# Two attentions: the split of one weight chunk moved behind the rotary embedding, and a value transposition moved ahead

## The chip, the cores and the metric

One Trainium2 chip, one NeuronCore of it. The metric is the device time of one execution in microseconds (us). The engines are named as in the profile: PE is TensorE's matmul, PEld its weight load, DVE is VectorE, ACT ScalarE, POOL GpSimd, and SP the engine that issues nearly all DMAs, one after the other. Each engine works through its own list of instructions in order and waits on semaphores where it needs another's result.

## What is computed

A decoder step of four layers for 256 prompt tokens and 64 sample tokens that share all weights (320 columns, 1024 features, float32). Each layer is a SwiGLU network, a token mixer, and another SwiGLU network, each behind an RMS norm. The mixers are a chunked gMLP, a sliding-window attention with sinks, a short convolution, and a sparse attention. The two attentions matter here:

```python
q = _rope(qkv[..., :qd]...)          # sliding-window attention: 16 heads, 2 key/value heads
k = _rope(qkv[..., qd:qd + kvd]...)
o, ... = _band_attn(q, k, v, window=128, sinks)
x = x + o @ w_o

proj = xn @ w_in                     # sparse attention
q, kv4, kvw, gates = ...             # kv4: k_cmp, v_cmp, k_sel, v_sel; kvw: k_win, v_win
q_rot = _rope(q); k_sel = _rope(k_sel); k_win = _rope(k_win)
o = gates0 * o_cmp(q) + gates1 * o_sel(q_rot) + gates2 * o_win(q_rot)
x = x + o @ w_o
```

For the samples, the sparse attention reads its past selected keys and values from a paged cache (8 pages for each of 8 sequences) and the last 128 window rows from another.

## The kernel before

All matrices of weights arrive as chunks of 1024 x 256 in one stream. SP loads chunk n into one of two slots of `w_raw` (L264), but only after the slot's former chunk, n - 2, has been split: `sp_chunk` waits on `lo_ready`. The split makes float32 out of two rounded parts: ACT copies a half chunk to `w_hi` (`act_split`, L290), DVE subtracts it from the raw values into `w_lo` (`dve_split`, L299, two instructions a chunk, one a half). PE then makes three products for each of eight row tiles of a half (`pe_half`, L317). ACT and DVE run two chunks ahead: while PE multiplies with chunk c of a stage, they split chunk c + 2. So in the last two chunks of an attention's input projection they split the first and the second chunk of the output projection (`mix_out`).

The projection of an attention (`pe_in_turning`, `dve_in_turning`) interleaves the rotary embedding with the chunks. DVE evacuates both halves of chunk c (`dve_take3`, L933), splits chunk c + 2, and then rotates the tiles of chunk c - 1 (`turned`). One rotation is: POOL multiplies by the cosine (L928), PE multiplies by a permutation into bank 5 or 6 (L884), DVE multiplies that by the sine (L907) and adds the cosine part (L910). After the last chunk two rotations of the chunk before it and two of its own are left.

After the projection come rounds: eight heads' pairs and eight sequences (`rounds`), in each of which three units u = 0, 1, 2 (two prompt tiles, one sequence) are scored, masked, exponentiated, turned and multiplied with values. POOL stages the queries (L1225 to L1239, L2025 to L2029) once the last rotation is through, PE makes the scores (L1066; L1687 to L1700), DVE masks them (from L1170; from L1899).

In the sparse attention PE, behind the last rotation, waits until DVE has read banks 5 and 6 (`rot_sin`), transposes the prompt's and the samples' new values of two branches into them (L1672, six transpositions), ACT copies them out (L1790, L1791), and PE waits for these copies (`nv_ready`) before its first scores. The gates and the compressed keys and values are laid out earlier with banks 7 and 4 (`lay`; DVE signals its end with five steps of `n_lay_step`).

SP's list around the sparse attention is: the eight chunks of `nsa_in`, the four chunks of `mix_out` (the fourth, chunk 3, waits for the split of the second, chunk 1), then `sp_nsa_store`: the window caches `n_wk` (L1601) and `n_wv` (L1602), then in a loop eight page numbers out of SBUF (L1607) and eight page loads into `n_sel` (L1611), for one sequence after the other. PE's unit u = 2 needs `n_wk` and `n_wv` from L1693 on and the pages from L1700 on. In the sliding-window attention the caches are loaded before the chunks of `mix_out`.

Of the kernel before, what the change touches and what calls it, by code (L numbers as in the profile page):

```python
# [10 lines left out]
ACT = mybir.ActivationFunctionType  # L11
# [3 lines left out]
P = 128  # L15
# [3 lines left out]
NS_TOK = 64  # L19
# [13 lines left out]
RAW = 2  # L33
# [73 lines left out]
def program(nc, A, O, schedule):  # L107

    ctx = ExitStack()
    with ctx:  # L110
# [90 lines left out]
        def cst(name):  # L201
            a, n = COLS[name]
            return const[:, a:a + n]
# [89 lines left out]
        def dve_split(dve, n, i=0, step=0, k=KT):  # L293

            one = n in narrow and not step
            for half in range(1 if one else 2):
                s = (2 * n + half) % HALVES
                dve.wait_ge(hi_ready, 2 * n + half + 1 + 2 * step * i)
                dve.tensor_tensor(w_lo[:, s, 0:k, :], raw[:, n % RAW, 0:k, P * half:P * half + P],  # L299
                                  w_hi[:, s, 0:k, :].bitcast(F32), ALU.subtract).then_inc(lo_ready, 2 if one else 1)  # L300
# [554 lines left out]
        if kinds & {"swa", "nsa"}:  # L855
            rot_turned = sem("rot_turned")
            rot_sin = sem("rot_sin")
# [18 lines left out]
        def pe_in_turning(pe, st, turns, between=None):  # L876

            n0, g0, norm = st["n0"], st["g0"], st["norm"]

            def turn(c):  # L880
                for r, src, _ in turns_of(turns, c):
                    pe.wait_ge(evacuated, g0 + turns[r][0] + 1)
                    pe.wait_ge(rot_sin, st["rope"] + r + 1)
                    pe.matmul(bank[5 + r % 2][:, 0:T], cst("perm"), flat1(src), start=True, stop=True).then_inc(rot_turned, 1)  # L884

            for c in range(st["chunks"]):
                one = n0 + c in narrow
                for half in range(1 if one else 2):
                    operand = (lambda k: pe.wait_ge(xlo_ready, KT * norm + k + 1)) if c == half == 0 else None
                    pe_half(pe, n0 + c, half, g0 + 2 * c + half, x_hi, x_lo, operand=operand).then_inc(half_used, 2 if one else 1)  # L890
                if c == 0:
                    pe_norm(pe, norm)
                turn(c - 1)
                if between and c in between:
                    between[c]()
            turn(st["chunks"] - 1)

        def dve_in_turning(dve, st, outs, turns, between=None):

            n0, g0 = st["n0"], st["g0"]  # L900

            def turned(c):
                for r, _, dst in turns_of(turns, c):
                    at = st["rope"] + r
                    dve.wait_ge(rot_turned, at + 1)
                    dve.wait_ge(rope_ready, at + 1)
                    dve.tensor_tensor(rot_s[:, r % 2, :], bank[5 + r % 2][:, 0:T], cst("sin"), ALU.mult).then_inc(rot_sin, 1)  # L907
                    dve.wait_ge(rot_sin, at + 3)
                    dve.wait_ge(rot_cos, at + 1)
                    dve.tensor_tensor(flat1(dst), rot_c[:, r % 2, :], rot_s[:, r % 2, :], ALU.add).then_inc(rope_ready, 1)  # L910

            dve_rstd(dve, st["norm"])
            for c in range(st["chunks"]):
                one = n0 + c in narrow
                for half in range(1 if one else 2):
                    dve_take3(dve, n0 + c, half, g0 + 2 * c + half, outs[2 * c + half], count=2 if one else 1)
                dve_split(dve, n0 + RAW + c)
                turned(c - 1)
                if between and c in between:
                    between[c]()  # L920
            turned(st["chunks"] - 1)
# [234 lines left out]

        def dve_swa(dve, st):
            dve_in_turning(dve, st, [at_kv[:, t:t + 1, :] for t in range(2)] + [at_q[:, t:t + 1, :] for t in range(KT)], swa_turns)
            dve.wait_ge(swa_landed, 48)
            dve.tensor_scalar(at_sink8[:, :], at_sink[:, :], 1.0 / SCALE, None, ALU.mult).then_inc(sink_ready, 1)  # L1160
            dve.wait_ge(sink_ready, 1)

            def stepped(u, r, m):

                dve.wait_ge(at_step[u], 3 * r + m)

            def mask(V, u, r, k):
                dve.wait_ge(s_ready, V)
                dve.wait_ge(pt_turned, V - 3)
                dve.memset(at_none[:, :], 0.0)  # L1170
                for grp in range(1 + (u < 2)):
                    if u < 2:
                        p, scored, seen = groups(u)[:, grp, :], scores_at(u, grp), cst("m_band")[:, P - P * u:2 * P]
                    else:
                        p, scored, seen = at_p[:, u, 0:KEYS[u]], bank[0][:, 0:KEYS[u]], at_msk[:, :]
                    m = dve.tensor_tensor_reduce(p, scored, seen, 1.0, at_snk[:, u, grp:grp + 1], ALU.add, ALU.max,
                                                 at_mx[:, u, grp:grp + 1])
                m.then_inc(masked, 1)

            def negate(V, u, r, k):  # L1180
                w = 1 + (u < 2)
                dve.wait_ge(masked, V)
                dve.tensor_scalar(at_neg[:, u, 0:w], at_mx[:, u, 0:w], -SCALE, None, ALU.mult).then_inc(neg_ready, 1)
                dve.tensor_tensor(at_esk[:, u, 0:w], at_snk[:, u, 0:w], at_mx[:, u, 0:w], ALU.subtract).then_inc(at_step[u], 1)

            def total(V, u, r, k):
                w = 1 + (u < 2)
                dve.wait_ge(exp_ready, V)
                dve.tensor_tensor(at_sum[:, u, 0:w], at_sum[:, u, 0:w], at_es[:, u, 0:w], ALU.add).then_inc(at_step[u], 1)
                stepped(u, r, 2)  # L1190
                dve.reciprocal(at_rec[:, u, 0:w], at_sum[:, u, 0:w]).then_inc(at_step[u], 1)

            def scale(V, u, r, k):
                stepped(u, r, 3)
                if u < 2:
                    p = groups(u)[:, 0, :]
                    o = dve.tensor_scalar(p, p, at_rec[:, u, 0:1], None, ALU.mult)
                else:
                    p = at_p[:, u, 0:KEYS[u]]
                    o = dve.tensor_scalar(p, p, at_rec[:, u, 0:1], None, ALU.mult)  # L1200
                o.then_inc(p_ready, 1)

            def remainder(V, u, r, k):
                dve.wait_ge(o_hi, V)
                if u < 2:
                    rows = slice(P * u, P * u + P)
                    o = dve.tensor_tensor(queries(h_lo, r, rows), out_bank[u][:, 0:P], queries(h_hi, r, rows).bitcast(F32),
                                          ALU.subtract)
                else:
                    for grp in range(2):  # L1210
                        o = dve.tensor_tensor(sample_rows(h_lo, grp, r), out_block(out_bank[u], grp),
                                              sample_rows(h_hi, grp, r).bitcast(F32), ALU.subtract)
                o.then_inc(o_lo, 1)

            rounds(dve, SWA_ROUND, dict(mask=mask, negate=negate, total=total, scale=scale, remainder=remainder))
            dve.wait_ge(o_lo, PRIME + 24)
            dve.nop().then_inc(mixer_ready, KT)
# [409 lines left out]
        def pe_nsa(pe, st):  # L1627
# [35 lines left out]
                    mm = pe.matmul(bank[4][0:64, 0:P], n_hid_of(1, k), w2z[:, 1, k // 2, k % 2, :], start=(k == 0), stop=(k == 3))  # L1663
                mm.then_inc(n_laid, 1)

            pe_in_turning(pe, st, nsa_turns, between={3: hidden, 4: turn_hidden, 5: lay})

            pe.wait_ge(rot_sin, 2 + st["rope"] + 10)
            for a in range(2):
                for c in range(3):  # L1670
                    w = P if c < 2 else NS_TOK
                    tr = pe.transpose(bank[5 + a][0:w, P * c:P * c + P], n_kv[:, 3 + 2 * a, P * c:P * c + w], cst("ident"))  # L1672
            tr.then_inc(nv_turned, 1)
            pe.wait_ge(n_lay_step, 5)
            pe.wait_ge(nv_ready, 4)

# [86 lines left out]
        def act_nsa(act, st):  # L1763
# [20 lines left out]
                    g_op.then_inc(nhid_gelu, 1)  # L1784
            for c in range(5, 8):
                act_split(act, st["n0"] + RAW + c)
            act.wait_ge(nv_turned, 1)
            act.wait_ge(evacuated, st["g0"] + st["groups"])
            for a in range(2):
                act.activation(n_vt[a][:, :, :], bank[5 + a][:, 0:2 * P].rearrange("p (c n) -> p c n", c=2), ACT.Copy).then_inc(nv_ready, 1)  # L1790
                act.activation(n_vs[a][:, :], bank[5 + a][0:NS_TOK, 2 * P:3 * P], ACT.Copy).then_inc(nv_ready, 1)  # L1791

            def exp_of(p, u, col):
                return act.activation(p, p, ACT.Exp, bias=n_neg[:, u, col:col + 1], scale=SCALE, accum_out=n_sum[:, u, col:col + 1])  # L1794
# [52 lines left out]
        def dve_nsa(dve, st):  # L1847
# [25 lines left out]
            dve.wait_ge(evacuated, st["g0"] + st["groups"])  # L1873
            dve.wait_ge(n_lay_step, 5)
            dve.wait_ge(rope_ready, 2 + st["rope"] + 10)

            def stepped(u, r, m):

# [417 lines left out]
```

## Time and profile before

| what | us |
|---|---|
| median of 3 runs | 2647.28 |
| lowest and highest of them | 2647.09 and 2649.73 |
| the profiled execution, its own time | 2643.24 |
| span of the profiled execution, first to last instruction | 2641.1 |

The profile is one execution, 4.0 us under the median of the runs. A line of a timeline gives the start and the length of a piece of work, its engine, its line and operands, its count (xN) and, in brackets, how long the engine had been idle and what it waited for. Overlapping pipelines make neighbouring instructions overlap by up to 0.1 us. In tables of stretches, PEclk is the granted clock of TensorE: 1.00 is its 2.4 GHz level, 0.50 the 1.2 GHz level.

### The profile page before, as it was taken

The page shows a single profiled execution, that of the slowest core. Times are in us where ns is not written, and L with a number is a line of the kernel's source. Part 1 is how long each engine was busy: PE and PEld are TensorE (multiplying, and loading weights), DVE is VectorE, ACT ScalarE, POOL GpSimd, SP SyncE. Part 2 cuts the span into 40 slices and gives each one's busy share as a digit, 9 for nine tenths or more (in the row PEclk, how much of TensorE's full clock was granted, in tenths as well). Part 3 has the DMA queues.
Part 4 walks back from the last instruction along what each step waited for, and adds up shares of the span by engine and source line. Part 5 has one row for each costly group of instructions (what it writes and reads, how often), then busy time and mean ns, then how long its engine had stood idle before and what let it go on. Part 6 is the DMA issues. An engine that isn't in the chain of part 4 may idle for free. (4 is left out here: it accounts for less than half of the span.)

```text
span 2641.1 us, 50131 instructions
## 1 busy us (share of the span) xinstructions
PE 2538.1 (96%) x17479; PEld 2471.5 (94%) x17479; DVE 1408.2 (53%) x2216; ACT 1331.9 (50%) x1995; POOL 767.8 (29%) x802
## 2 busy tenths in 40 slices
PE   6999998999999998999999999999999997889998
PEld 6999997999999985999999998999999996669997
DVE  6454545554454466645455456654545446756553
ACT  4565443564465336555366332554466334755542
POOL 2333213333133222333133224332233211113331
PEclk8999998999999998999999999999999998889999
DMA  6234342444444440343444443444444353214432
GB/s 220 91 129 154 135 158 97 159 143 144 149 153 153 148 178 2 145 158 135 151 159 143 148 155 121 151 146 149 151 153 149 144 206 115 61 48 146 156 139 104
DMA packets 66302, 366.20 MB, mean 139 GB/s; under 512 B 9154, under 2 KB 21762, under 8 KB 28290
## 3 DMA queue, kind: packets, MB, share of 16 engines
q1 hardware_dynamic: 64530, 356.58, 37.5%
q0 software_dynamic: 1536, 4.20, 0.5%
q10 hardware_dynamic: 144, 4.19, 0.4%
q8 instruction: 58, 0.95, 0.1%
q14 instruction: 34, 0.28, 0.0%
HBM read 361.98 MB, written 4.92 MB: 139 GB/s over the span
## 5 line engine op out<-in xcount | busy, mean ns | idle before, releaser
L317 PE MATMUL bank<-x_hi,w_hi 128*128 128x320 f32 x3336 | 1035.1, 310 | 0.0
L290 ACT ACTIVATE w_hi<-w_raw 128x1024 fp32r<-128x1024 f32 (+1 forms) x641 | 657.8, 1036 | 741.7 <-PE bank L317 718.2
L317 PE MATMUL bank<-x_lo,w_hi 128*128 128x320 f32 x3336 | 1030.9, 309 | 0.0
L317 PE MATMUL bank<-x_hi,w_lo 128*128 128x320 f32 x3336 | 1030.8, 309 | 0.0
L299 DVE TENSOR_TENSOR w_lo<-w_raw,w_hi 128x1024 fp32r<-128x1024 f32 (+1 forms) x641 | 828.8, 1328 | 258.3 <-ACT w_hi L290 258.3
L317 PEld LDWEIGHTS bank<-x_hi,w_hi 128*128 128x128 f32 x3336 | 626.2, 188 | 1.9 <-issue 0.6
L317 PEld LDWEIGHTS bank<-x_hi,w_lo 128*128 128x128 f32 x3336 | 626.2, 188 | 1.3
L317 PEld LDWEIGHTS bank<-x_lo,w_hi 128*128 128x128 f32 x3336 | 626.1, 188 | 0.0
L317 PE MATMUL bank<-h_hi,w_hi 128*128 128x320 f32 x1664 | 517.8, 311 | 8.4 <-POOL h_lo L843 6.1
L317 PE MATMUL bank<-h_hi,w_lo 128*128 128x320 f32 x1664 | 516.8, 311 | 0.0
L317 PE MATMUL bank<-h_lo,w_hi 128*128 128x320 f32 x1664 | 516.6, 310 | 0.0
L501 POOL TENSOR_TENSOR h<-silu,up 128x320 f32<-128x320 f32 x176 | 222.2, 1263 | 846.9 <-DVE up L430 846.8
L317 PEld LDWEIGHTS bank<-h_hi,w_hi 128*128 128x128 f32 x1664 | 314.7, 189 | 9.8 <-POOL h_lo L843 7.0
L317 PEld LDWEIGHTS bank<-h_hi,w_lo 128*128 128x128 f32 x1664 | 314.8, 189 | 0.0
L317 PEld LDWEIGHTS bank<-h_lo,w_hi 128*128 128x128 f32 x1664 | 314.7, 189 | 0.0
L488 POOL TENSOR_TENSOR sq<-x 128x320 f32 (+1 forms) x104 | 82.4, 792 | 594.0 <-DVE x L450 593.3
L430 DVE TENSOR_TENSOR up<-bank,rstd 128x320 f32<-128x320 f32 x176 | 86.3, 492 | 302.7 <-PE bank L317 302.7
L430 DVE TENSOR_TENSOR gate_in<-bank,rstd 128x320 f32<-128x320 f32 x192 | 93.5, 491 | 271.1 <-PE bank L317 262.7
L506 POOL TENSOR_TENSOR h_lo<-h,h_hi 128x320 f32 x176 | 237.3, 1367 | 0.0
L375 ACT ACTIVATE x_hi<-x,gains (+1 forms) x96 | 53.4, 563 | 206.5 <-DVE x L450 206.5
L391 ACT ACTIVATE h_hi<-h 128x320 f32 x176 | 81.7, 464 | 96.4 <-POOL h L501 96.3
L290 ACT ACT_TABLE_LOAD x90 | 115.5, 1283 | 15.9 <-DMA w_raw<-stream 14.4
(284 smaller groups left out, 2000.3 us busy)
## 6 DMA issues: line engine op xcount, KB each, us to landing
w_raw<-stream SPq DMA_DIRECT2D x289, 1024.0 KB, 4.8
w_raw<-stream SPq DMA_DIRECT2D x32, 768.0 KB, 4.1
n_sel<-pool_sel SPq DMA_DIRECT2D x64, 128.0 KB, 2.2
w_raw<-cmp_w SPq DMA_DIRECT2D x4, 1024.0 KB, 9.8
pages<-pool_cmp SPq DMA_DIRECT2D x32, 128.0 KB, 4.8
pages<-pool_cmp POOLq DMA_DIRECT2D x32, 128.0 KB, 5.1
w_new<-cmp_w ACTq DMA_DIRECT2D x1, 4096.0 KB, 13.6
const<-const SPq DMA_DIRECT2D x1, 1533.0 KB, 10.6
```

The costliest lines, as they stand in the source:

```text
L290: act.activation(w_hi[:, (2 * n + half) % HALVES, 0:k, :], raw[:, n % RAW, 0:k, P * half:P * half + P], ACT.Copy).then_inc(hi_ready, 2 if ...
L299: dve.tensor_tensor(w_lo[:, s, 0:k, :], raw[:, n % RAW, 0:k, P * half:P * half + P], w_hi[:, s, 0:k, :].bitcast(F32), ALU.subtract).then_i ...
L317: mm = pe.matmul(acc, w[:, s, kk, :], a[:, k0 + kk, :], start=(first and kk == 0 and w is w_hi and a is act_hi), stop=(last and kk == k - ...
L375: act.activation(x_hi[:, bass.ds(m, 1), :], x[:, bass.ds(m, 1), :], ACT.Copy, scale=gains[:, norm, bass.ds(m, 1)]).then_inc(xhi_ready, 1)
L391: act.activation(h_hi[:, bass.ds(2 * i + f, 1), :], h[:, f:f + 1, :], ACT.Copy).then_inc(hhi_ready, 1)
L430: dve.tensor_tensor(dst, bank[g % BANKS][:, 0:T], rstd[:, :], ALU.mult).then_inc(evacuated, 1)
L488: pool.tensor_tensor(sq[:, :].rearrange("p (a t) -> p a t", a=1), x[:, bass.ds(m, 1), :], x[:, bass.ds(m, 1), :], ALU.mult).then_inc(ssum_ ...
L501: pool.tensor_tensor(h[:, f, :], silu[:, f, :], up[:, f, :], ALU.mult).then_inc(prod_ready, 1)
L506: pool.tensor_tensor(h_lo[:, t, :], h[:, f:f + 1, :], h_hi[:, t, :].bitcast(F32), ALU.subtract).then_inc(hlo_ready, 1)
```

## The change

In both attentions DVE no longer splits the last of the two chunks ahead (the second chunk of `mix_out`) between the evacuation of the last projection chunk and the last four rotations. In the sliding-window attention the split now stands after the rotations and the scaling of the sinks, ahead of the rounds; in the sparse attention after DVE's wait for the last rotation, ahead of the rounds. In the sparse attention PE transposes the values after the first two of the last four rotations' matmuls (it waits there for `n_lay_step`), into banks 7 and 4 in place of 5 and 6, and ACT copies each bank when its own three transpositions are done. Ahead of the rounds PE waits for the last rotation (`rope_ready`) where it waited for DVE's last read of bank 6.

```diff
@@ dve_in_turning
                     dve_take3(dve, n0 + c, half, g0 + 2 * c + half, outs[2 * c + half], count=2 if one else 1)
-                dve_split(dve, n0 + RAW + c)
+                if c < st["chunks"] - 1:
+                    dve_split(dve, n0 + RAW + c)
                 turned(c - 1)
@@ dve_swa
             dve.tensor_scalar(at_sink8[:, :], at_sink[:, :], 1.0 / SCALE, None, ALU.mult).then_inc(sink_ready, 1)
+            dve_split(dve, st["n0"] + RAW + st["chunks"] - 1)
             dve.wait_ge(sink_ready, 1)
@@ pe_nsa
-            pe_in_turning(pe, st, nsa_turns, between={3: hidden, 4: turn_hidden, 5: lay})
-
-            pe.wait_ge(rot_sin, 2 + st["rope"] + 10)
-            for a in range(2):
-                for c in range(3):
-                    w = P if c < 2 else NS_TOK
-                    tr = pe.transpose(bank[5 + a][0:w, P * c:P * c + P], n_kv[:, 3 + 2 * a, P * c:P * c + w], cst("ident"))
-            tr.then_inc(nv_turned, 1)
+            def turn_values():
+                pe.wait_ge(n_lay_step, 5)
+                for a in range(2):
+                    for c in range(3):
+                        w = P if c < 2 else NS_TOK
+                        tr = pe.transpose(bank[(7, 4)[a]][0:w, P * c:P * c + P], n_kv[:, 3 + 2 * a, P * c:P * c + w], cst("ident"))
+                    tr.then_inc(nv_turned, 1)
+
+            pe_in_turning(pe, st, nsa_turns, between={3: hidden, 4: turn_hidden, 5: lay, 7: turn_values})
+            pe.wait_ge(rope_ready, 2 + st["rope"] + 10)
             pe.wait_ge(n_lay_step, 5)
             pe.wait_ge(nv_ready, 4)
@@ act_nsa
-            act.wait_ge(nv_turned, 1)
             act.wait_ge(evacuated, st["g0"] + st["groups"])
             for a in range(2):
-                act.activation(n_vt[a][:, :, :], bank[5 + a][:, 0:2 * P].rearrange("p (c n) -> p c n", c=2), ACT.Copy).then_inc(nv_ready, 1)
-                act.activation(n_vs[a][:, :], bank[5 + a][0:NS_TOK, 2 * P:3 * P], ACT.Copy).then_inc(nv_ready, 1)
+                act.wait_ge(nv_turned, a + 1)
+                act.activation(n_vt[a][:, :, :], bank[(7, 4)[a]][:, 0:2 * P].rearrange("p (c n) -> p c n", c=2), ACT.Copy).then_inc(nv_ready, 1)
+                act.activation(n_vs[a][:, :], bank[(7, 4)[a]][0:NS_TOK, 2 * P:3 * P], ACT.Copy).then_inc(nv_ready, 1)
@@ dve_nsa
             dve.wait_ge(rope_ready, 2 + st["rope"] + 10)
+            dve_split(dve, st["n0"] + RAW + st["chunks"] - 1)
```

## Rows read from the trace of the kernel before

**Rows 1.** Page, part 1: busy time, share of the span, instructions of each engine.

```profile
PE 2538.1 (96%) x17479; PEld 2471.5 (94%) x17479; DVE 1408.2 (53%) x2216; ACT 1331.9 (50%) x1995; POOL 767.8 (29%) x802
```

**Rows 2.** Stretches, sparse attention: length, busy (count) per engine, PEclk, DMA share, GB/s.

```profile
2206.00:2208.00 2.00, 0.79 (x3) 0.34 (x3) 1.93 (x5) 0.00 (x0) 0.41 (x1) 1.00 0.24 33
2208.00:2210.00 2.00, 1.40 (x2) 0.46 (x2) 1.97 (x3) 0.00 (x0) 1.33 (x2) 0.50 0.85 340
...
2224.00:2226.00 2.00, 2.00 (x6) 0.87 (x6) 0.05 (x1) 0.19 (x2) 0.00 (x0) 0.74 0.30 90
...
2230.00:2235.00 5.00, 4.16 (x44) 3.24 (x41) 4.43 (x26) 2.63 (x6) 0.00 (x0) 1.00 0.00 0
```

**Rows 3.** Timeline of DVE, sparse attention: start, length, engine, line, work, idle before.

```profile
2204.16 2.35 DVE L299 TENSOR_TENSOR w_lo<-w_raw,w_hi 128x1024 fp32r<-128x1024 f32 x2
2206.43 0.48 DVE L907 TENSOR_TENSOR gate_in<-bank,const 128x320 f32<-128x320 f32 x1
...
2208.73 0.48 DVE L907 TENSOR_TENSOR gate_in<-bank,const 128x320 f32<-128x320 f32 x1
...
2210.60 0.49 DVE L910 TENSOR_TENSOR n_qr<-up,gate_in 128x320 f32<-128x320 f32 x1
2215.25 0.22 DVE L1899 TENSOR_TENSOR n_p<-bank,const 128x64 f32<-128x64 f32 x1 [4.16 <-PE bank L1689]
```

**Rows 4.** Timeline of PE, sparse attention, without the projection's matmuls.

```profile
2203.56 1.24 PE L884 MATMUL bank<-n_q,const 128*128 128x320 f32 x4
2207.06 0.78 PE L884 MATMUL bank<-n_q,const 128*128 128x320 f32 x2 [2.27 <-DVE gate_in L907]
...
2210.63 1.54 PE L1672 MATMUL bank<-const,n_kv 128*128 128x128 f32 x6 [1.23 <-DVE gate_in L907]
2213.28 1.22 PE L1687 MATMUL bank<-n_kv,n_qst 64*128 64x128 f32 x8 [1.11 <-ACT n_vs L1791]
...
2221.05 0.66 PE L1693 MATMUL bank<-n_kv,n_qss 128*128 128x64 f32 x2 [1.89 <-issue]
...
2222.77 3.07 PE L1700 MATMUL bank<-n_sel,n_qss 128*128 128x512 f32 x4
```

**Rows 5.** Timeline of SP's DMA issues, sparse attention.

```profile
2206.69 0.33 SPq L264 DMA_DIRECT2D w_raw<-stream  x1
...
2214.31 0.36 SPq L1611 DMA_DIRECT2D n_sel<-pool_sel  x1
...
2217.95 0.33 SPq L1611 DMA_DIRECT2D n_sel<-pool_sel  x1
```

**Rows 6.** Waits of SP from 2200 to 2222 us: total, times, longest.

```profile
SPq L264 <- DVE w_lo L299: 7.5, 1, 7.5
```

**Rows 7.** Tile n_sel, its first eight issues (2213 to 2219 us).

```profile
DMA to landing us min/median/max: 2.0/2.2/2.4
```

**Rows 8.** Timeline of POOL, sparse attention: the first and last of six stagings.

```profile
2211.22 0.29 POOL L2025 COPY n_qst<-n_q 128x128 f32<-128x128 f32 x1 [1.41 <-issue]
...
2212.55 0.41 POOL L2029 TENSOR_TENSOR n_qss<-n_qr,const 128x128 f32<-128x128 f32 x1
```

**Rows 9.** Lines L299 and L928, 2176 to 2210 us: ns min/median/max, starts.

```profile
L299 DVE TENSOR_TENSOR w_lo<-w_raw,w_hi x8: 1215/1217/1911, 2177.4 to 2205.3; 128x1024 fp32r<-128x1024 f32 x8
...
L928 POOL TENSOR_TENSOR up<-n_q,const x7: 863/890/1800, 2177.6 to 2209.0; 128x320 f32<-128x320 f32 x7
```

**Rows 10.** Timeline of DVE, sliding-window attention.

```profile
981.97 2.35 DVE L299 TENSOR_TENSOR w_lo<-w_raw,w_hi 128x1024 fp32r<-128x1024 f32 x2
984.24 0.48 DVE L907 TENSOR_TENSOR gate_in<-bank,const 128x320 f32<-128x320 f32 x1
...
988.83 0.17 DVE L1160 TENSOR_SCALAR at_sink<-at_sink 128x17 f32<-128x17 f32 x1
990.85 0.06 DVE L1170 MEMSET at_none<- 128x1 f32 x1 [1.85 <-issue]
```

**Rows 11.** Timeline of PE, sliding-window attention: the first scores.

```profile
989.93 1.66 PE L1066 MATMUL bank<-at_kv,at_qst 64*128 64x128 f32 x8 [2.94 <-POOL at_snk L1233]
```

## The prediction

> **What bounds the kernel now.** I read the page's busy shares first: PE is at work for 96% of the span [rows 1], so an edit elsewhere counts only where PE stands still or runs slowly. The changed code touches two such places, the passages from an attention's projection to its rounds. Next I read the timelines of all engines there, and the stretches for the granted clock.
>
> In the sparse attention PE is through with the projection at about 2203.6. DVE then splits a weight chunk from 2204.16 to 2206.43, 2.27 us [rows 3], while PE has two rotations' matmuls left and then stands idle for 2.27 us [rows 4]. Four rotations follow on DVE without a gap, from 2206.43 to 2211.09: 4.66 us [rows 3]. The six transpositions come behind DVE's last read, take 1.54 us, and the first scores start at 2213.28 on ACT's release [rows 4]. DVE has been idle 4.16 us when it masks at 2215.25 [rows 3]. The reader is to see a serial chain, DVE, PE, ACT, PE, with a split in it that nobody on it needs. In the sliding-window attention it is the same without the transpositions: split 981.97 to 984.24, rotations and sinks until about 989.0, idle 1.85 us, mask at 990.85 [rows 10].
>
> The third thing to read is who does need the split. SP does: its wait before L264 is ended by the DVE split, after 7.5 us [rows 6]. It issues that weight load at 2206.69, 0.26 us behind the split's end, and everything else on its list stands behind it: the window caches, eight page numbers, and the first page load at 2214.31, the eighth at 2217.95 [rows 5]. This landed 2.0 to 2.4 us later [rows 7], at 2219.95 to 2220.35. PE reads these pages at 2222.77 without an idle mark on that row [rows 4]; the slack is 2.4 to 2.8 us, 2.6 in the middle.
>
> **The change in the sliding-window attention.** Nothing is added; the split moves behind the sinks. The rotations then start when the last evacuation and PE's first remaining permutation are through, 2.2 us earlier than 984.24, and the sinks end at 986.8 instead of 989.0. From there two things run side by side. Staging and scores took 1.85 us between sinks and mask (PE began at 989.93 on POOL's release [rows 11]): ready at 988.65. The split takes 2.27 us alone: ready at 989.05. The split is late last, so the cover is not quite enough. But it now runs beside POOL's staging. A split half took 1.22 us in the middle of eight and 1.91 us at most, when a POOL multiplication at the same time took 1.80 instead of 0.89 [rows 9]: 0.69 us for one collision, which I take because it is the same instruction against the same engine. The ends are 0 and the whole of the six stagings of the sparse attention, 2211.22 to 2212.96, 1.74 us [rows 8]. The mask then starts at 989.05 to 990.8, with 0.69 at 989.75: gain 0.1 to 1.8, taken **1.1 us**. SP's later load of weight chunk 3 costs nothing here: the caches of this attention stand ahead of it in the list, and the load is needed only when the output projection starts, behind all rounds.
>
> The Trainium skill, page "SBUF — State Buffer", section "Who interferes with whom", says that a VectorE instruction with two SBUF inputs contends with a GpSimd instruction that reads SBUF, by an exclusive lock. The collision row agrees. If every staging locked the split out, this would be the upper end: hardly a gain here, and 1.05 us more lost below, in sum 2651.7 instead of 2649.6.
>
> **The change in the sparse attention, up to the second scores.** The permutations of the first two remaining rotations end at 2203.56 + 1.24 = 2204.80, the first of them at about 2204.2 [rows 4]; DVE starts there. PE then transposes. DVE wants the third permutation 2208.73 - 2206.43 = 2.30 us into its rotations [rows 3], at 2206.5. At the price of the row, 2204.80 + 1.54 + 0.78 = 2207.12, it is 0.6 late; but that row lies where the clock was 0.50, and it was 1.00 until 2208 [rows 2]. At half the time it is ready at 2206.35. Bounds 0 and 0.6; taken 0, since the stretch right behind the projection is the nearest. The rotations end at 2204.2 + 4.66 = 2208.9, 2.2 us earlier. ACT's copies are done by then, hidden behind the rotations. PE's new wait for the last rotation has only scores behind it, which need POOL's staging after it anyway. POOL stages, PE scores, DVE splits from 2208.9 to 2211.2, with 0.69 of collision to 2211.9 (up to 2213.5 with both bounds). The mask could start there instead of at 2215.25: **3.3 us earlier**, and the samples' scores as much.
>
> **The change in the sparse attention, from SP's side.** The moved split signals SP at 2211.9 instead of 2206.43, 5.4 us later (4.7 to 7.1, the last with both bounds). Each step of SP's list up to the eighth page load is as long as before, 2217.95 - 2206.43 = 11.5 us, since none waits for an engine: page numbers and issues are SP's own work. So the pages land at 2225.5 instead of 2220.15. PE, ready for them 3.3 us earlier, at 2219.5, has little but idle time until then (its four small products ahead of L1700 wait for the window caches, which move with the list too) and starts L1700 at about 2225.6 instead of 2222.77. The loss is 5.4 less the slack of 2.6: **2.8 us** (4.7 - 2.8 = 1.9 to 7.1 - 2.4 = 4.7). PE's turn of the first unit is queued behind L1700, so are DVE's masking and ACT's copies of the samples' scores. The pages of the next sequence move too, but have the length of a round to do so.
>
> Last the clock. L1700 took 3.07 us, and the mean of 0.74 over 2224 to 2226 means that the clock rose at about 2225.04, in its course [rows 2]: 0.8 us of it ran at full clock. After six idle us it would start at 0.50. It loses up to 0.8 us, and the turn behind it as much again at most: 0 to 1.5, taken **0.6 us**, nearer to the lower end since the row's own rise came 2.3 us into the same work.
>
> **Sum.** -1.1 + 2.8 + 0.6 = +2.3 us. Against the profiled execution's own 2643.24 that is 2645.5; that execution lies 4.0 us under the median of the runs, and measured times are compared by medians: 2647.28 + 2.3 = **2649.6**. From the bounds, -1.8 + 1.9 + 0 = +0.1 to -0.1 + 4.7 + 1.5 = +6.1; the ends seldom meet, and the runs shown differ by 2.6 us: 2645.5 to 2653.5 for this case.
>
> **The rivals.** *The pages aren't late.* If SP's list doesn't hold PE up, both passages keep their gains: -1.1 - 3.3 = -4.4, 2642.9. For it speaks that every other step of the chain shortens; against it that SP's wait row names the very split and that the slack is half of the delay. If besides PE's filled gap held the clock at 1.00, the half-clock stretch from 2208 to 2225 would cost some 4 us less: from the first scores at 2213.28 to L1700's end at 2225.84 [rows 4] lie 12.6 us, PE works in an estimated two thirds of them, and that would halve: 2638.9. *The clock stays down (slower).* The place is the first full round behind the late L1700. If the idle us ahead of it put the rise off by a round, matmuls that now take 4.16 of 5 us at clock 1.00 [rows 2] would run at 0.50; for some 5 us of them half of the doubling shows, +2 to +3, and with the 4.7 end of the late pages: -1.1 + 4.7 + 2.5 = +6.1, 2653.4 and up. It decides from a loss of 5.3 us on. *The two attentions cancel:* little collision gives -1.8 + 1.9 = +0.1, 2647.4; it lies within the forecast.
>
> **How the numbers follow.** A median of this kernel can tell about 0.2%, 5.3 us, from no change: below 2642.0 is faster, above 2652.6 slower. Chances: the forecast 0.72 (in it 0.06 over 2652.6); the clock stays down or the late pages cost their upper end 0.14, of which 0.11 over the bound; the pages aren't late 0.14, of which 0.07 under the bound. That gives faster 0.07, same 0.76, slower 0.17. The range takes in the forecast's ends and half of each neighbour: 2643.5 to 2654.0.
>
> **What would show it.** Right: in the profile of the changed kernel the last rotation of the sparse attention ends some 2.2 us sooner after the projection, the transpositions stand between permutations, the first mask follows the split; SP's weight load follows the later split, the eighth page load, issued 14.4 us behind the projection's end before (2217.95 against 2203.56), is issued about 19.8 us behind it; and PE is idle several us ahead of L1700. In the sliding-window attention the mask begins right behind the split. Wrong: L1700 without an idle gap (the pages weren't late), a first mask well behind the split (another wait), or a clock that never falls in the passage.

## The result

The changed kernel takes 2650.06 us, median of 20 runs (2645.84 to 2654.09); the kernel before took 2645.47 in 20 runs beside it (2640.43 to 2651.67). The ratio is 1.0017, with a 95% interval of 1.0009 to 1.0025: 4.5 us slower, between 2.4 and 6.6. The predicted 2649.6 is 0.5 us off as a time, but it was reckoned from a median of three runs that lay 1.8 us above that of all twenty; as a difference, +2.3 was forecast and +4.5 measured. The sign was right and the size half of it; that the time itself came so close is luck. One of 33 executions of the kernel before, on the chip of the first four experiments, took 4386.92 us and is left out of their ratios.

The profiled execution of the changed kernel has a span of 2645.9 us (before 2641.1). Its chain that ended last has two new members, SP's queue and a DMA, each with less than half a per cent of the span. Page, part 4, engines, before and after:

```profile
PE 13%; DVE 2%; ACT 1%; issue 1%; DVEq 0%; POOL 0%; ACTq 0%; POOLq 0%
PE 11%; DVE 2%; ACT 1%; issue 1%; SPq 0%; DVEq 0%; DMA 0%; POOL 0%; ACTq 0%; POOLq 0%
```

Line numbers moved by up to five in the changed file: the transpositions are L1673, the first scores L1691, the samples' scores L1697 to L1704, the page loads L1613. Clock times of the two profiles can't be compared directly, so every time below is counted from PE's first late permutation: 2203.56 before [rows 4], 2206.38 after. PE's timeline in the sparse attention of the changed kernel:

```profile
2206.38 1.24 PE L884 MATMUL bank<-n_q,const 128*128 128x320 f32 x4
2207.45 0.82 PE L1673 MATMUL bank<-const,n_kv 128*128 128x128 f32 x6
2208.11 1.35 PE L884 MATMUL bank<-n_q,const 128*128 128x320 f32 x4
2213.80 1.22 PE L1691 MATMUL bank<-n_kv,n_qst 64*128 64x128 f32 x8 [4.35 <-POOL n_qst L2031]
...
2222.24 0.66 PE L1697 MATMUL bank<-n_kv,n_qss 128*128 128x64 f32 x2 [2.59 <-DMA n_wv<-win_v]
...
2229.16 3.78 PE L1704 MATMUL bank<-n_sel,n_qss 128*128 128x512 f32 x4 [4.98 <-DMA n_sel<-pool_sel]
```

PE now closes its idle gap with the transpositions, and gains at the first scores: 7.42 us behind the first late permutation instead of 9.72. Then it waits twice for DMAs that it did not wait for before, 2.59 us for the window values and 4.98 us for the pages. L1704 begins at 22.78 us instead of 19.21: 3.57 us later. It also takes 3.78 us instead of 3.07; whether that comes of the wait is looked at below.

Why the pages come late stands on DVE's and SP's timelines, and in SP's waits from 2206 to 2230:

```profile
2206.57 0.49 DVE L934 TENSOR_TENSOR n_q<-bank,rstd 128x320 f32<-128x320 f32 x1 [1.31 <-PE bank L317]
2207.11 0.49 DVE L907 TENSOR_TENSOR gate_in<-bank,const 128x320 f32<-128x320 f32 x1
...
2211.31 0.49 DVE L910 TENSOR_TENSOR n_qr<-up,gate_in 128x320 f32<-128x320 f32 x1
2212.00 2.52 DVE L299 TENSOR_TENSOR w_lo<-w_raw,w_hi 128x1024 fp32r<-128x1024 f32 x2 [0.20 <-DVE n_qr L910]
2215.75 0.22 DVE L1904 TENSOR_TENSOR n_p<-bank,const 128x64 f32<-128x64 f32 x1 [1.23 <-PE bank L1693]
```

```profile
2214.69 0.33 SPq L264 DMA_DIRECT2D w_raw<-stream  x1
2215.24 0.34 SPq L1603 DMA_DIRECT2D n_wk<-win_k  x1
...
2222.32 0.89 SPq L1613 DMA_DIRECT2D n_sel<-pool_sel  x2
...
2226.25 0.85 SPq L1613 DMA_DIRECT2D n_sel<-pool_sel  x2
```

```profile
SPq L264 <- DVE w_lo L299: 12.7, 1, 12.7
```

The eight page loads as a group, each one's ns min/median/max and the first and last start:

```profile
L1613 SPq DMA_DIRECT2D n_sel<-pool_sel x8: 332/333/1135, 2222.3 to 2226.8; - x8
```

The rotations follow the last evacuation at once, and the split ends at 2214.5. SP's wait for it has grown from 7.5 [rows 6] to 12.7 us. Up to the first page load SP's list behind the wait is as long as ever: 7.63 us from the weight load, 7.62 before [rows 5]. It has moved by 5.2 us against the projection's end.

The stretches of the changed kernel show the clock in this passage (columns as in [rows 2]):

```profile
2206.00:2210.00 4.00, 3.45 (x18) 2.23 (x16) 3.27 (x7) 3.00 (x6) 1.24 (x2) 1.00 0.00 0
2210.00:2214.00 4.00, 0.20 (x2) 0.23 (x4) 3.76 (x5) 0.31 (x1) 2.60 (x4) 0.95 0.00 0
...
2226.00:2230.00 4.00, 0.83 (x1) 0.50 (x2) 0.00 (x0) 0.00 (x0) 0.00 (x0) 0.50 0.46 144
2230.00:2234.00 4.00, 4.00 (x9) 1.73 (x7) 0.90 (x7) 1.02 (x2) 0.78 (x2) 0.50 0.10 30
2234.00:2238.00 4.00, 2.62 (x24) 2.05 (x25) 3.49 (x16) 1.98 (x10) 0.00 (x0) 0.99 0.78 232
```

It holds at 1.00 longer behind the projection, where PE is now at work for 3.45 of 4 us, but falls all the same once PE is idle, and is at 0.50 through the whole of L1704, where in the profile of the kernel before it rose in its course [rows 2].

The sliding-window attention gained next to nothing. DVE, POOL and PE of the changed kernel there, each from its own timeline:

```profile
987.92 2.35 DVE L299 TENSOR_TENSOR w_lo<-w_raw,w_hi 128x1024 fp32r<-128x1024 f32 x2
991.73 0.06 DVE L1172 MEMSET at_none<- 128x1 f32 x1 [1.46 <-issue]
```

```profile
988.14 1.04 POOL L1227 COPY at_snk<-at_sink 128x1 f32<-128x1 f32 x1 [1.50 <-DVE at_sink L1161]
989.12 1.30 POOL L1233 COPY at_qst<-at_q 128x128 f32<-128x128 f32 x1
990.37 0.18 POOL L1235 COPY at_snk<-at_sink 128x2 f32<-128x2 f32 x1
990.49 0.29 POOL L1233 COPY at_qst<-at_q 128x128 f32<-128x128 f32 x1
```

```profile
982.50 2.15 PE L884 MATMUL bank<-at_q,const 128*128 128x320 f32 x6
...
990.81 1.66 PE L1067 MATMUL bank<-at_kv,at_qst 64*128 64x128 f32 x8 [5.23 <-POOL at_snk L1235]
```

PE's first late permutation before, from the timeline of the kernel before:

```profile
981.36 1.24 PE L884 MATMUL bank<-at_q,const 128*128 128x320 f32 x4
```

From there to the first mask it took 990.85 - 981.36 = 9.49 us before [rows 10] and takes 991.73 - 982.50 = 9.23 after: 0.26 us gained of the 2.1 by which the rotations came earlier. While the two halves of the split run, two of POOL's staging copies take 1.04 and 1.30 us; once it is over, a copy of the same shape takes 0.29. PE waits for them. DVE, through with the split at 990.27, starts its mask 0.92 us behind PE's first scores, as before (989.93 and 990.85): it waits for PE.

### The profile page after: what moved, and what is told of

The parts are those of the page before. It is cut to its first block and busy times, and to the rows that moved or that the text cites. A ratio compares the mean times of both kernels' runs of the same rounds, so it can differ in the third digit from the quotient of the medians.

```text
span 2645.9 us, 50133 instructions
## 1 busy us (share of the span) xinstructions
PE 2532.0 (96%) x17479; PEld 2468.1 (93%) x17479; DVE 1408.8 (53%) x2216; ACT 1331.4 (50%) x1995; POOL 771.2 (29%) x802
## 5 line engine op out<-in xcount | busy, mean ns | idle before, releaser
L299 DVE TENSOR_TENSOR w_lo<-w_raw,w_hi 128x1024 fp32r<-128x1024 f32 (+1 forms) x641 | 828.8, 1328 | 258.6 <-ACT w_hi L290 258.4
L450 DVE SCALAR_TENSOR_TENSOR x<-bank,x 128x320 f32 (+1 forms) x96 | 47.0, 490 | 145.3 <-PE bank L317 145.3
```

The source lines that it names most:

```text
L450: dve.scalar_tensor_tensor(out=xm, in0=bank[g % BANKS][:, 0:T].rearrange("p (a t) -> p a t", a=1), scalar=scale, in1=xm, op0=ALU.mult, op1 ...
```

## The experiments

The theory: the loss sits in the sparse attention, because SP's list waits for the moved split and the pages arrive late. The rivals: DVE and POOL blocking each other costs the time; the moved transpositions or the clock that they change cost it; or the order of SP's loads is a matter of its own. All kernels compute everything. Each ratio is against runs of the kernel before on the same chip.

**The split moved in the sliding-window attention alone.**

```diff
-                dve_split(dve, n0 + RAW + c)
+                if c < st["chunks"] - 1 or st["kind"] != "swa_in":
+                    dve_split(dve, n0 + RAW + c)
@@ dve_swa, behind the scaling of the sinks
+            dve_split(dve, st["n0"] + RAW + st["chunks"] - 1)
```

> The split is moved in the sliding-window attention alone; the sparse attention is as before. Late-pages theory: the whole loss of the change lies in the sparse attention, so this kernel loses nothing: from the last evacuation of the projection to the first mask 9.0 us as with the whole change (9.3 before), POOL's first staging copies stretched from 0.2 and 0.3 to over 1 us by the split, and in the sparse attention 19.2 us from PE's first late permutation to L1700 as before; time -0.3 us against before, not to be told from 0. Port-lock rival (the loss of the change comes from POOL and DVE blocking each other in both attentions): slower than before by 1 us or more.

2645.22 us, ratio 0.9998 (0.9988 to 1.0008): no difference. The first mask comes 9.19 us behind the first late permutation, L1702 (the L1700 of before) 19.20. POOL's first two copies take 1.04 and 1.30 us, as with the whole change. This part neither loses nor gains anything that can be measured; the blocking eats the gain but is not the loss.

**The split moved in the sparse attention alone.**

```diff
-                dve_split(dve, n0 + RAW + c)
+                if c < st["chunks"] - 1 or st["kind"] != "nsa_in":
+                    dve_split(dve, n0 + RAW + c)
@@ dve_nsa
             dve.wait_ge(rope_ready, 2 + st["rope"] + 10)
+            dve_split(dve, st["n0"] + RAW + st["chunks"] - 1)
```

> The split is moved in the sparse attention alone; the transpositions stay behind the last rotation, the sliding-window attention is as before. Late-pages theory: the split's end moves 5 us or more behind the projection's end, SP's list with it, PE waits several us for the pages of n_sel and L1700 starts 22.5 to 23.5 us behind the first late permutation instead of 19.2; time +3.5 to +5 us, as much as the whole change. Rival (the transpositions between the rotations, or the clock they change, cost the time): no loss here, or a gain of 1 to 2 us.

2648.97 us, ratio 1.0014 (1.0004 to 1.0023): 3.7 us slower, 1.1 to 6.1. PE's timeline of this kernel:

```profile
2200.05 2.15 PE L884 MATMUL bank<-n_q,const 128*128 128x320 f32 x6
...
2215.89 0.66 PE L1694 MATMUL bank<-n_kv,n_qss 128*128 128x64 f32 x2 [2.74 <-DMA n_wv<-win_v]
...
2222.11 2.93 PE L1701 MATMUL bank<-n_sel,n_qss 128*128 128x512 f32 x3 [4.28 <-DMA n_sel<-pool_sel]
```

The window of this view ends within L1701; its four matmuls take 3.78 us, as with the whole change. The same two waits stand here with the transpositions at their old place. L1701 begins 22.06 us behind the permutation, a little under the expected 22.5. The split alone makes the loss, as closely as the two intervals can tell; the rival of the transpositions falls.

**The transpositions moved alone** (the parts of the change in `pe_nsa` and `act_nsa`, both splits at their old places).

> The transpositions are moved alone; both splits stand where they stood before. Late-pages theory: SP's list is as before, so the pages land in time (slack 2.6 us), first scores wait for POOL's staging instead of ACT's copies and come 1.4 us earlier, L1700 starts 17.8 us behind the first late permutation instead of 19.2, no wait for pages; time -1.4 us. Rival (the transpositions cost the time): L1700 later than 19.2 us and the time up by some us.

2644.06 us, ratio 0.9992 (0.9982 to 1.0001): 2.1 us faster by the middle, from 4.8 faster to 0.3 slower. In its profile the scores wait for POOL, not for ACT, and the pages keep no one waiting:

```profile
2202.91 1.24 PE L884 MATMUL bank<-n_q,const 128*128 128x320 f32 x4
...
2211.43 1.22 PE L1689 MATMUL bank<-n_kv,n_qst 64*128 64x128 f32 x8 [3.31 <-POOL n_qst L2028]
...
2220.93 3.02 PE L1702 MATMUL bank<-n_sel,n_qss 128*128 128x512 f32 x4
```

L1702 begins at 18.02 us instead of 19.21: 1.2 us, close to the 1.4 expected. The passage shows the gain, the time does not resolve it.

**The whole change, with the caches and pages ahead of the fourth weight chunk in SP's list.**

```diff
             for st in stages:
+                if st.get("mixer") == "nsa":
+                    for c in range(3):
+                        sp_chunk(sp, st["n0"] + c)
+                    sp_nsa_store(sp)
+                    sp_chunk(sp, st["n0"] + 3)
+                    continue
                 sp_stream(sp, st)
```

> The whole change, but SP loads the window caches and all pages ahead of the fourth chunk of the sparse attention's output projection, so that they no longer stand behind the moved split. Late-pages theory: no wait for pages, L1700 starts 2 to 3 us earlier than before, at 16.5 to 17 us behind the first late permutation (after: 22.8); the time is 5 to 7 us under the changed kernel and 2 to 3 under the kernel before. Port-lock rival: the order of the loads doesn't matter, L1700 stays at 22 to 23 us and the time within 1 us of the changed kernel.

2640.42 us, ratio 0.9980 (0.9968 to 0.9992): 5.3 us faster than before, 2.1 to 8.5. Its medians beside their own runs of before (2640.42 against 2645.27, 2650.06 against 2645.47) put it some 9 us under the changed kernel. PE's timeline:

```profile
2206.16 1.24 PE L884 MATMUL bank<-n_q,const 128*128 128x320 f32 x4
...
2213.59 1.23 PE L1691 MATMUL bank<-n_kv,n_qst 64*128 64x128 f32 x8 [4.35 <-POOL n_qst L2031]
...
2223.28 3.73 PE L1704 MATMUL bank<-n_sel,n_qss 128*128 128x512 f32 x4
```

No wait for a DMA is left; L1704 begins at 17.12 us (expected 16.5 to 17), 2.1 earlier than before and 5.7 earlier than with the change as made. The time fell by more than expected, 5.3 us where 2 to 3 were, and exceeds this passage's 2.1 and the sliding-window attention's 0.3; the interval reaches down to 2.1, and what lies above 2.4, if it is real, is not explained.

**The kernel before with that order of loads alone.**

> The kernel before with SP's order alone changed: window caches and pages of the sparse attention ahead of the fourth chunk of the output projection. Late-pages theory: in the kernel before the pages had 2.6 us of slack, so the order alone gives nothing: L1700 19.2 us behind the first late permutation as before, time within 1 us of before. Rival (the order of the loads is a gain of its own, and the changed kernel with this order only borrows it): L1700 1 us or more earlier and the time 2 us or more down.

2644.58 us, ratio 1.0002 (0.9993 to 1.0011); its L1700 begins 19.24 us behind the permutation, where it was 19.21. The order gives nothing by itself, as the pages had slack before. That rival falls too.

**Both splits moved on, out of POOL's staging,** with pages first. Of the diff the new places are shown; at the places of the change the splits are taken out.

```diff
@@ dve_swa, step scale: behind the last scaling of the first look-ahead
+                if u == 2 and isinstance(r, int) and r == 0:
+                    dve_split(dve, st["n0"] + RAW + st["chunks"] - 1)
@@ dve_nsa, step mask: ahead of the first sequence's mask
+                if u == 2 and isinstance(r, int) and r == 0:
+                    dve_split(dve, st["n0"] + RAW + st["chunks"] - 1)
```

> The changed kernel with SP's order of the kernel with pages first, and with both moved splits moved on: in the sparse attention to the place ahead of DVE's mask of the first sequence's scores, in the sliding-window attention behind the last scaling of the first look-ahead, so that neither runs beside POOL's staging. Port-lock theory: POOL's first staging copies take 0.2 to 0.3 us instead of 1.0 to 1.3; the first mask of the sliding-window attention comes 7.2 us behind the first late permutation instead of 9.2 (9.5 before), and L1700 16 us behind it instead of 17.1; of the 2.0 us won in the sliding-window attention the split takes back about 1.3 after the first look-ahead. Time 3.5 to 5 us under before. Rival (the split's place beside the staging doesn't matter): masks at 9.0 us and later, L1700 at 17 us, time as with pages first alone.

2639.32 us, ratio 0.9976 (0.9967 to 0.9986): 6.3 us faster than before, 3.7 to 8.7, where 3.5 to 5 were expected. POOL and DVE of this kernel in the sliding-window attention:

```profile
986.91 0.19 POOL L1228 COPY at_snk<-at_sink 128x1 f32<-128x1 f32 x1 [1.49 <-DVE at_sink L1161]
987.03 0.29 POOL L1234 COPY at_qst<-at_q 128x128 f32<-128x128 f32 x1
```

```profile
988.63 0.06 DVE L1171 MEMSET at_none<- 128x1 f32 x1 [1.85 <-issue]
...
993.37 2.35 DVE L299 TENSOR_TENSOR w_lo<-w_raw,w_hi 128x1024 fp32r<-128x1024 f32 x2
```

With no split beside them the two copies take 0.19 and 0.29 us instead of 1.04 and 1.30, and the first mask comes 7.3 us behind the first late permutation: the full 2.1 us. In the sparse attention L1705 (the L1704 of the change) begins at 15.8 us, 1.3 earlier than with the split beside the staging. So the blocking is shown, and its price up to these points: about 1.9 us in the one passage, 1.3 in the other. What of it reaches the time is not: against pages first alone the two times can't be told apart (intervals 0.9968 to 0.9992 and 0.9967 to 0.9986).

## Why the prediction came out as it did

**What bounds it, and SP's side: right.** That the split has a second reader, SP, and that the page loads stand behind it, was read from the wait row and held. The pages' delay was forecast as 5.4 us less a slack of 2.6. Measured: SP's weight load 5.2 us later against the projection; from the first page load to the eighth 4.4 us instead of 3.6, as one of the issues took 1.1 us where the others take 0.3. The pages cost 3.57 us at L1700, forecast 2.8 (1.9 to 4.7). I had called every step of the list as long as before; one was not, and why is not known.

**The clock term: the number came, the reason is not shown.** L1704 ran wholly at 0.50 and took 3.78 us, +0.71; from its start to the first unit's values the stretch grew from 5.02 to 5.83 us, by 0.8, forecast 0.6 (0 to 1.5). I had put this down to the idle time ahead of L1704. But two kernels that have this passage as it was before, without a wait for pages, ran the same work as slowly. The split moved in the sliding-window attention alone, and the order of loads alone:

```profile
2228.19 3.73 PE L1702 MATMUL bank<-n_sel,n_qss 128*128 128x512 f32 x4
```

```profile
2224.96 3.73 PE L1700 MATMUL bank<-n_sel,n_qss 128*128 128x512 f32 x4
```

In both the stretch up to the first unit's values is 5.77 us. So the 0.8 us are for the most part a difference between single executions, the profile of the kernel before being one in which the clock rose early, and that they agree with the forecast is luck. Whether the change lowers the clock in other rounds is open. A hint is there: the runs of the sparse split alone had a granted clock of 0.9717 in the mean of 12, those of the kernel before 0.9735 in the mean of 32 on the same chip, while single runs spread from 0.969 to 0.977.

**The rotations and transpositions: right.** The last rotation ends 5.42 us behind the first late permutation, 7.53 before: 2.1 us sooner, forecast 2.2. The six transpositions took 0.82 us at full clock, forecast half of 1.54, and the third rotation did not wait for them.

**The sliding-window attention: the step that was mis-sized.** I took 1.1 us of gain; it is 0.26. The step took the collision as one stretch of the split, 0.69 us, from a row in which a split half and a POOL multiplication had both grown. In fact the split kept its 2.35 us and POOL's copies took all the delay, and these copies stand between the rotations and the first scores. I had reckoned the split late last; staging and scores were. The same mistake stands in the sparse attention, where I forecast a first mask 3.3 us earlier, right behind the split: it was 2.3 earlier and waited 1.23 us for PE, which waited for POOL. There it cost nothing, since the pages came later still.

The Trainium skill, page "SBUF — State Buffer", section "Who interferes with whom", says that the port pair that the two engines share is an exclusive lock and that the issue order decides who blocks. The trace agrees: the split began at 987.92 and the first copy at 988.14, so the split held the port, and a copy of 0.29 us took 1.30. In the prediction this rule gave the upper end, hardly a gain, with the staging locking the split out; 0.26 us of gain came, but with the split locking the staging out, so that the size came right and the order did not. For the sum I had turned the lock into a stretch of the wrong engine.

Corrected, the sum is -0.26 + 3.57 = +3.3 us, or +4.1 with the 0.8 that the change need not have caused; both lie inside the measured 2.4 to 6.6. That these delays reach the end of the attention whole is not shown. From the first late permutation to the first matmul of the output projection one execution took 160.85 us before (to 2364.41) and one 162.26 after (to 2368.64), only 1.4 more; with the sparse split alone it took 165.56. The rounds between vary by more than the effect, as the last section shows, so the loss rests on the times and its cause on the waits.

Of the rivals, the late pages that don't matter fell with the wait of 4.98 us. Nor did the two attentions cancel: the one gained 0.26 us, the other lost more. The clock that stays down for a round did not come: it was back at 0.99 in the mean of the stretch from 2234, in the same round.

## What to carry to other kernels

Before moving a step off a chain, look up every engine that waits for its signal, the one that issues DMAs above all: here a split of 2.3 us set the time of a list of issues and loads some 13.5 us long. When two engines are to run side by side, ask which of them holds the shared resource first and whether the other one's delay lies on the chain; here it was not a stretch shared between them. And a moved wait in a list of issues is mended by what stands behind it: loads that don't need the signal go ahead.

## What the runs showed of the hardware

Single executions of one kernel spread over 11 us (2640.43 to 2651.67 in 20 runs of the kernel before), four times what its first three runs had shown. The spread goes with the clock, as every run has its mean granted clock on record. Of 32 runs of the kernel before on the chip of the first four experiments, the five at 0.970 or less took 2649.44 to 2651.37 us, the twelve at 0.975 or more 2637.33 to 2646.89.

Within one profile it shows in the rounds. Two rounds of the sparse attention in the kernel before, each from the start of one L1700 to the next (columns as in [rows 2]):

```profile
2307.08:2326.37 19.29, 17.30 (x138) 13.23 (x138) 12.99 (x64) 12.23 (x48) 2.48 (x7) 0.73 0.18 54
2326.37:2342.34 15.97, 13.07 (x139) 9.89 (x138) 12.78 (x65) 12.29 (x47) 2.43 (x7) 1.00 0.38 129
```

With nearly the same number of matmuls the one took 19.29 us at a mean clock of 0.73, the other 15.97 at 1.00. Why a round runs at the one or the other in one execution and not in the next was not tried.

The second thing is who pays when DVE and POOL block each other. In the sliding-window attention the split had begun first and kept its 2.35 us, while POOL's copies took four to five times their length. It is not always POOL that pays: in [rows 9] a POOL multiplication that began at 2177.55, behind the first half of a split at 2177.39, took 1.80 us instead of 0.89, and the second half behind it took 1.91 instead of 1.22.
